# Stick-breaking attention on TensorE: the first key sum goes ahead of a transpose, the sample's scores behind the second sum

## What is computed

```python
def one_block(args):
    q_blk, start = args
    z = jnp.einsum('bqhd,bkhd->bhqk', q_blk, k).astype(jnp.float32) * scale
    q_pos = q_offset + start + jnp.arange(blk)
    before = key_pos[None, :] < q_pos[:, None]
    log_1m_beta = jnp.where(before, jax.nn.log_sigmoid(-z), 0.0)
    log_after = lax.cumsum(log_1m_beta, axis=3, reverse=True) - log_1m_beta
    weights = jnp.where(before, jnp.exp(jax.nn.log_sigmoid(z) + log_after), 0.0)
    return jnp.einsum('bhqk,bkhd->bqhd', weights.astype(v.dtype), v)
```

## Time and profile before

| what | value |
|---|---|
| device time, median of 3 runs | 2138.4 us (2130.19, 2138.4, 2140.45) |
| profiled execution, its own time | 2125.48 us |
| profiled execution, its span | 2123.8 us |
| mean granted TensorE clock in it | 0.981 |
| TensorE busy in the span | 2000.0 us (94%) |
| VectorE busy | 1155.2 us (54%) |
| ScalarE busy | 546.1 us (26%) |

### The profile page before, as it was taken

One profiled execution on the slowest core, in us unless ns is written; L12 is line 12 of the kernel. 1 busy time (PEld: TensorE's weight loads), 2 busy tenths in 40 slices (PEclk: granted clock), 3 DMA queues, 4 the chain that ended last, 5 costly groups with the idle time before them and its releaser, 6 DMA issues. The chain is left out here.

```text
span 2123.8 us, 46388 instructions
## 1 busy us (share of the span) xinstructions
PE 2000.0 (94%) x20494; PEld 1878.0 (88%) x20494; DVE 1155.2 (54%) x1593; ACT 546.1 (26%) x1012; POOL 203.3 (10%) x289
## 2 busy tenths in 40 slices
PE   8998998998999999996999988879999999999998
PEld 8997778996999999995898867668998899999997
DVE  5336775554655555336656744427655565555433
ACT  2005774113210010000236543334212211010111
POOL 5000001000200000010000245420010100000000
PEclk9999999999999999997999999999999999999999
DMA  4234212352232232232121000014341222333222
GB/s 133 80 122 142 60 31 70 121 154 73 80 89 82 86 89 87 82 91 81 50 80 58 19 4 5 4 47 117 110 159 50 60 86 83 89 89 88 82 82 79
DMA packets 299360, 169.75 MB, mean 80 GB/s; under 512 B 10328, under 2 KB 294176, under 8 KB 299200
## 3 DMA queue, kind: packets, MB, share of 16 engines
q1 hardware_dynamic: 294976, 151.25, 24.5%
q10 hardware_dynamic: 4224, 16.12, 2.0%
HBM read 155.94 MB, written 11.41 MB: 79 GB/s over the span
## 5 line engine op out<-in xcount | busy, mean ns | idle before, releaser
L259 PE MATMUL psum<-words_r,weights_high_r 128*128 128x272 f32 (+1 forms) x7808 | 1495.1, 291 | 11.1 <-DVE words_r L210 3.7
L259 PEld LDWEIGHTS psum<-words_r,weights_high_r 128*128 128x128 f32 x7808 | 1232.1, 189 | 22.9 <-issue 18.9
L259 PE MATMUL psum<-words_r,weight_ring_r 128*128 128x272 f32 (+1 forms) x3904 | 1130.3, 290 | 0.0
L259 PEld LDWEIGHTS psum<-words_r,weight_ring_r 128*128 128x128 f32 x3904 | 737.5, 189 | 0.0
L205 DVE TENSOR_SCALAR weights_high_r<-weight_ring 128x1024 fp32r<-128x1024 f32 (+1 forms) x258 | 177.9, 690 | 523.1 <-PE psum L259 519.1
L210 DVE TENSOR_TENSOR weight_ring_r<-weight_ring,weights_high_r 128x1024 fp32r<-128x1024 f32 (+1 forms) x264 | 319.4, 1210 | 11.2 <-ACT weights_high_r L344 2.4
L399 POOL TENSOR_TENSOR words<-words,words 128x544 f32<-128x544 f32 x35 | 61.6, 1759 | 1046.7 <-ACT words L386 1046.7
L1973 ACT ACTIVATE words<-words 128x544 f32<-128x544 f32 x44 | 29.0, 659 | 451.7 <-DVE words L1901 451.7
L2744 PE MATMUL psum<-words 64*64 64x64 f32 (+1 forms) x3168 | 90.4, 235 | 19.6 <-issue 16.4
L2744 PEld LDWEIGHTS psum<-words 64*64 64x64 f32 x3168 | 71.3, 135 | 34.5 <-issue 31.6
L210 DVE TENSOR_TENSOR words_r<-words,words_r 128x544 fp32r<-128x544 f32 (+5 forms) x124 | 88.3, 720 | 8.2 <-ACT words_r L331 2.6
(11 more groups left out here) (338 smaller groups left out, 1929.2 us busy)
## 6 DMA issues: line engine op xcount, KB each, us to landing
weight_ring<-in_ffn_w_gate_up_dram SPq DMA_DIRECT2D x88, 512.0 KB, 3.8
weight_ring<-in_xa_w_kv_dram SPq DMA_DIRECT2D x32, 512.0 KB, 3.9
weight_ring<-in_ffn_w_down_dram SPq DMA_DIRECT2D x32, 448.0 KB, 3.4
weight_ring<-in_sb_w_qkv_dram SPq DMA_DIRECT2D x24, 512.0 KB, 3.8
weight_ring<-in_xa_w_q_dram SPq DMA_DIRECT2D x16, 512.0 KB, 3.7
weight_ring<-in_xa_w_o_dram SPq DMA_DIRECT2D x16, 512.0 KB, 3.6
weight_ring<-in_ffn_w_down_dram SPq DMA_DIRECT2D x16, 512.0 KB, 3.6
weight_ring<-in_sb_w_o_dram SPq DMA_DIRECT2D x8, 512.0 KB, 3.6
```

The source lines that it names most:

```text
L259: last = nc.tensor.matmul(c.psum[0:job.m(u), job.bank(q) + h, 0:w], weights[:, k, :], x[:, k, h * w:(h + 1) * w], start=job.opens(u) and k ...
```

## The change

In TensorE's list, `sum_x(p, 0)` goes ahead of `turn_past(p, 1)`, and `scores_s(p)` goes behind `sum_y(p, 0)`. No instruction is added or removed, and the lists of the other engines stay as they are. The diff is whole:

```diff
@@ -1130,10 +1130,10 @@
             scores_y(0)
             turn_past(0, 0)
             for p in range(PAIRS):
+                sum_x(p, 0)
                 turn_past(p, 1)
-                sum_x(p, 0)
+                sum_y(p, 0)
                 scores_s(p)
-                sum_y(p, 0)
                 sum_x(p, 1)
                 sum_y(p, 1)
                 if p + 1 < PAIRS:
```

## The result

The changed kernel takes 2166.1 us (median of 4 runs, 2162.7 to 2169.5) against 2135.6 us (median of 4 runs of before). The ratio is 1.0147, with a 95% interval of 1.013 to 1.0164: 1.5% slower. The profiled execution took 2162.7 us.

What follows compares the result with a forecast made beforehand. The prediction took TensorE, busy 94% of the span, to bound the kernel, in a tight ring with VectorE and ScalarE in attention. Schedule 15.0 plus clock 5.6 made 20.6 us, added to 2138.4 for 2159.0 us; range 2145 to 2170.

Steps and rivals of the forecast that it cites:

- Steps 1 to 4: TensorE's order in a pair: 0.90 us wait goes, about 2.0 us wait comes before the y sum, 1.49 us lost.
- Step 5: Work queued behind the late scores on VectorE and ScalarE: next pair's scores_x starts late, 1.81 us a pair lost in all.
- Step 6: Sample's sum_s and the loads behind the late scores: nothing added in seven pairs, 2.31 us in the last pair.
- schedule's sum of 15.0: Attention stage's loss from the order, without the clock: 7 x 1.81 + 2.31 = 15.0 us slower.
- Step 7: TensorE's clock lowered by the new wait in half the pairs: 4 pairs at 1.4 us, 5.6 us in all.
- bound of 1.7: Highest price in us of a lowered clock in one pair; 13.6 us if all eight pairs paid it.
- Rival C: Clock falls in every pair: 15.0 + 8 x 1.4 = 26.2 us slower, 2164.6 us; chance 0.15.
- Rival A: The schedule's loss with no lowered clock but where it is now: 15.0 us slower, 2153.4 us; chance 0.20.
- Rival B: TensorE's own order only, other two lists no gate: 1.49 us a pair, 11.9 in all, 2150.3 us; chance 0.08.
- Rival D: Not slower: if y0's low part lands by 207.64, each pair gains 0.70 us, 5.6 faster, 2132.8 us; chance 0.04.

Runs made afterwards that it cites:

- second set of runs: The changed kernel itself, unaltered, run once more beside the kernel before: 2159.4 us against 2134.1, ratio 1.0118.
- low_first: Against the changed kernel, VectorE's low part of y1 moved ahead of its cap of the sample's scores: one run of 2160.0 us.
- filled: Against the changed kernel, 16 more matmuls of 256 columns in each pair, ahead of the first y sum: 2148.5 us, ratio 1.0059.
- x_split: Against the kernel before, first x sum cut: high-part matmuls ahead of the second half's transposes, low-part ones behind: 2132.1 us, then 2126.8 us.
- copy_late: Against the changed kernel, ScalarE's copy of the second half of past keys moved behind its high parts of y0 and x1: 2141.1 us, ratio 1.0025.
- the shifted one: Against the changed kernel, 1.85 us more TensorE work in the second pair alone, ahead of its second half's transposes: 2171.5 and 2164.6 us.

## Why the prediction was right, and where its size was off

The direction, the mechanism and the range held; the size was 20.6 us against 30.5 (25.2 in the second set of runs).

**Steps 1 to 4** held to 0.02 us each. The wait of 0.90 us went, and one of 1.93 came where 1.94 was worked out.

**Step 5** held. `low_first` showed that ScalarE's list is the gate. A pair costs 1.87 us where I had 1.81; the row of `scores_x` is 0.05 later than worked out.

**Step 6** held: `sum_s` waits for nothing in the full-clock pairs, and the last pair is 2.34 us longer where the clock stays up (21.80 in `filled` against 19.46), forecast 2.31. The schedule's sum of 15.0 is thus 15.3 by the rows.

**Step 7** is the term that was mis-sized. I took four pairs at 1.4 us, 5.6 in all; in the changed kernel it is 27.4 - 15.3 = 12.1 us. The number of pairs was nearly right, five, but that was luck: "half" had no row behind it, and its reason, that the engine works fully on both sides of the wait, is true of every pair and so picks none. The price was wrong: three pairs pay 1.6 us, but the first pays 2.9 (25.0 - 20.2 - 1.9) and the seventh 4.4. The first pair's 2.9 is the least certain, since that pair's length varied by 4.0 us between the two executions of `x_split`. My bound of 1.7 came from the last pair of before, and supposed that the clock comes back as soon as it did there. In the seventh pair a mean of 0.79 over 24.03 us is some 10 us at half clock (24.03 x 0.21 / 0.5), with TensorE busy for 9.00 of 9.00 us in the longer stretch shown. In the third pair the same sum gives 3.4 us (21.18 x 0.08 / 0.5), and the price is 1.6. Rival C's all eight pairs did not come, but its 26.2 us is nearer to the stage's 27.4 than the forecast.

**Rival A** is the kernel `filled`: what the schedule costs when the clock stays up, 16.4 us of stage. Its argument "every pair at 1.00 now" overlooked the first pair, which ran at a mean of 0.77 from 185.0 to 195.7 us before the change. **Rival B** is refuted by the period, 1.87 us longer at full clock and not 1.49, and by `low_first`, where `scores_x` waits for the weights behind the sample's exp and log. **Rival D** had its deciding point right: the low part of y0 landed 1.5 us later than it would have had to. Even with the copy out of the way (`copy_late`) it is about 0.7 us too late (a wait of 1.1 where 1.93 - 1.49 = 0.44 could be afforded), and that kernel too is slower than before.

The Trainium skill, TensorE: Matmul & The Clock Gate, in its table under "Why this matters for your kernels", warns only of idle gaps longer than any of these. By itself that advice would have kept the forecast at 15.0, and this kernel does not bear it out: with waits of 1.9 us the clock was lowered in four or five of the seven pairs after the first, in each profile with such waits, and `filled`, without them, ran at 1.00. What the Trainium skill says on the same page under "PE-mode transpose", that transposes don't count as work for the clock as matmuls do, stays open; no run here replaced the transposes by other work.

The base was off by a few us as well, in the other direction: I added to a median of 2138.4, and later medians of the kernel before are 2131.9 to 2135.6. That offset brought the forecast 2159.0 nearer to the measured 2166.1 than its sum was, which is luck too.

## What to carry to other kernels

When an instruction moves across another on one in-order engine, write down for both when their inputs land and who is queued behind their outputs: here the moved work had been the cover for somebody else's chain, and moving it uncovered 1.9 us to fill 0.9. To fill a wait, cut the next ready piece to the wait's size (`x_split`), rather than move a whole step across a handoff. And price a new wait on TensorE with the clock it can cost: the same waits with filler work in them were 11 us cheaper in all.

## What the runs showed that was not expected

- TensorE's clock can stay at its lower level through long stretches in which the engine is busy all the time (9.00 of 9.00 us in the changed kernel's seventh pair, 10.00 of 10.00 in the first pair of `x_split`, which has no wait of 1.9 us), so a lowered clock cost 1.6 us in some pairs and 4.4 in another. What decides between these is not settled by these runs.
- Two executions of one program showed the same long pairs to within 0.1 us (the changed kernel), and two of another did not (the shifted one). A clean-looking pattern in one profile isn't yet a property of the kernel.
- Adding 128 matmuls in waits made a kernel faster: 2159.4 us for the changed kernel, 2148.5 with them, on one chip.
